# First modulation before the first FFN, the other seven vectors summed during it

## The reference

```python
m_lat = (jax.nn.silu(c) @ w_mod[l] + b_mod[l]).reshape(B, 1, N_MOD, D_MODEL)
m_ctx = (jax.nn.silu(c_ctx) @ w_mod[l] + b_mod[l]).reshape(N_MOD, D_MODEL)
def half_ffn(h, mod, i, g, w_up, w_down):
    shift, scale, gate = mod[..., 3 * i, :], mod[..., 3 * i + 1, :], mod[..., 3 * i + 2, :]
    return h + 0.5 * gate * swiglu(modulate(rms_norm(h, g), shift, scale), w_up, w_down)
h = half_ffn(h, m_lat, 0, g_norm[l, 0], w_ffn_up[l, 0], w_ffn_down[l, 0])
hc = half_ffn(hc, m_ctx, 0, g_norm[l, 0], w_ffn_up[l, 0], w_ffn_down[l, 0])
n_lat = modulate(rms_norm(h, g_norm[l, 1]), m_lat[..., 3, :], m_lat[..., 4, :])
h = h + m_lat[..., 5, :] * merge_branches(...)
h = half_ffn(h, m_lat, 2, g_norm[l, 2], w_ffn_up[l, 1], w_ffn_down[l, 1])
```

## Time and profile before

| | us |
|---|---|
| median of 3 runs | 3064.5 |
| lowest, highest | 3062.27, 3064.74 |
| profiled execution: span from first to last instruction | 3062.6 |
| TensorE busy in it | 2882.0 (94%) |
| DVE busy | 1494.6 (49%) |
| ScalarE busy | 556.8 (18%) |
| GpSimd busy | 69.0 (2%) |
| TensorE's mean granted clock | 0.959 |

### The profile page before, as it was taken

The page is one execution under the profiler, slowest core; times in us unless marked ns, Lnnn a source line. Parts: engine busy times, 40 slices in busy tenths (PEclk is TensorE's granted clock), DMA queues, the critical chain, the costliest instruction groups (busy, mean ns, idle before and its releaser), DMA issues. The chain is left out here.

```text
span 3062.6 us, 35904 instructions
## 1 busy us (share of the span) xinstructions
PE 2882.0 (94%) x14410; PEld 2300.6 (75%) x14410; DVE 1494.6 (49%) x2399; ACT 556.8 (18%) x1039; POOL 69.0 (2%) x104
## 2 busy tenths in 40 slices
PE   8999999999999999999956859998999999999998
PEld 3588888888888787888245637776877888888887
DVE  5544444444444711111696378886745444444444
ACT  3200000000000411111422337774011000000002
POOL 0000000000000000000000001221000000000001
PEclk9999999999999999999875669999999999999999
DMA  8511111111111211233400100001430111111111
GB/s 290 164 35 42 34 41 34 41 34 41 34 41 42 77 43 42 86 97 104 141 1 1 42 0 1 1 1 63 129 119 28 48 48 48 48 48 44 46 55 69
DMA packets 190653, 176.15 MB, mean 58 GB/s; under 512 B 5805, under 2 KB 147290, under 8 KB 190554
## 3 DMA queue, kind: packets, MB, share of 16 engines
q1 hardware_dynamic: 184794, 164.29, 17.3%
q10 hardware_dynamic: 5760, 10.49, 0.9%
HBM read 155.89 MB, written 18.87 MB: 57 GB/s over the span
## 5 line engine op out<-in xcount | busy, mean ns | idle before, releaser
L209 PE MATMUL psum<-nh,wh 128*128 128x512 f32 (+2 forms) x1688 | 613.3, 363 | 1.9 <-DVE wl L186 1.4
L210 PE MATMUL psum<-nl,wh 128*128 128x512 f32 (+2 forms) x1688 | 612.9, 363 | 0.0
L211 PE MATMUL psum<-nh,wl 128*128 128x512 f32 (+2 forms) x1688 | 612.5, 363 | 0.0
L184 DVE CAST wh<-raw 128x1024 fp32r<-128x1024 f32 x175 | 120.2, 687 | 707.8 <-PE psum L211 696.7
L209 PEld LDWEIGHTS psum<-nh,wh 128*128 128x128 f32 (+1 forms) x1688 | 317.1, 188 | 54.2 <-DVE wl L186 1.8
L211 PEld LDWEIGHTS psum<-nh,wl 128*128 128x128 f32 (+1 forms) x1688 | 316.8, 188 | 51.2
L210 PEld LDWEIGHTS psum<-nl,wh 128*128 128x128 f32 (+1 forms) x1688 | 317.1, 188 | 50.6
L717 DVE SCALAR_TENSOR_TENSOR h<-psum,gates,h 128x512 f32<-128x512 f32 (+1 forms) x400 | 271.0, 696 | 143.6 <-PE psum L211 140.5
L209 PE MATMUL psum<-hidh,wh 128*128 128x512 f32 (+1 forms) x880 | 328.2, 373 | 8.0 <-DVE hidl L701 7.6
L685 ACT ACTIVATE silu_a<-psum 128x512 f32<-128x512 f32 (+1 forms) x110 | 61.2, 556 | 1489.9 <-PE psum L211 1489.9
L210 PE MATMUL psum<-hidl,wh 128*128 128x512 f32 (+1 forms) x880 | 324.8, 369 | 0.0
(11 more groups left out here) (241 smaller groups left out, 3399.1 us busy)
## 6 DMA issues: line engine op xcount, KB each, us to landing
raw<-in_w_ffn_up_dram SPq DMA_DIRECT2D x88, 512.0 KB, 3.8
mod_raw<-in_w_mod_dram SPq DMA_DIRECT2D x24, 1024.0 KB, 5.2
raw<-in_w_ffn_down_dram SPq DMA_DIRECT2D x44, 512.0 KB, 3.8
raw<-in_w_in_dram SPq DMA_DIRECT2D x34, 512.0 KB, 3.8
mod_raw_late<-in_w_mod_dram SPq DMA_DIRECT2D x12, 1024.0 KB, 5.2
gates_saved<-staged ACTq DMA_DIRECT2D x40, 256.0 KB, 2.0
merge_gate<-gates_saved SPq DMA_DIRECT2D x8, 1024.0 KB, 5.1
x_rows<-in_x_dram SPq DMA_DIRECT2D x8, 512.0 KB, 7.2
```

The lines of the kernel that those rows point to most:

```text
L184: nc.vector.tensor_copy(wh[:, par, 0:n], raw[:, par, 0:n]).then_inc(panel_split, 1)
L209: pe.matmul(o, hi_w, hi_x, start=first, stop=False)
L210: pe.matmul(o, hi_w, lo_x, start=False, stop=False)
L211: return pe.matmul(o, lo_w, hi_x, start=False, stop=last)
```

## The change

Only the first four blocks (vectors 0 and 1: shift and scale of the first FFN, both samples) are still multiplied by TensorE ahead of the FFN, in eight slots that need no waiting. The norm moves behind them, and the first panels are split before it, so that TensorE's pairs follow the norm block by block. The other seven vectors (e = 0 to 6, numbers 2 to 8) are made by GpSimd in groups 0 to 6 of the first FFN: SP loads 16 parts of 128 x 512 for a vector, GpSimd scales each by silu(c) per partition and adds it up, for vectors e = 0 to 2 also for the context; then TensorE sums the 128 partitions with matmuls against a column of ones, at the head of the group's down panels, and DVE adds the bias (`part_sums`, `part_finish`). Semaphores are shared with later stages, the vector loads move to ScalarE's queue, and the constants of later stages load later. The blocks in the GLA stage are gone. In after's code the L numbers are higher (L184 is L192, L209 is L217, L418 is L502, L428 is L512, L717 is L819).

```diff
--- before.py
+++ after.py
...
-    mod_raw = [at("mod_raw0", 120, [4, 512]), at("mod_raw1", 128, [4, 512]), at("mod_raw2", 164, [4, 512])]
-    mod_raw_late = [at("mod_raw_late0", 140, [4, 512]), at("mod_raw_late1", 172, [4, 512]),
-                    at("mod_raw_late2", 164, [4, 512])]
-    mod_row = at("mod_row", 201, [2, 512])
+    mod_raw = [at(f"mod_raw{n}", kb, [4, 512]) for n, kb in enumerate((120, 128, 164, 80, 88, 96, 104, 112))]
+    mod_row = at("mod_row", 193, [2, 512])
+    acc_lat, acc_ctx = at("acc_lat", 174, [D]), at("acc_ctx", 197, [D])
+    mod_part = [at(f"mod_part{n}", kb, [512]) for n, kb in enumerate((201, 203, 205, 186.5))]
+    part_prod = at("part_prod", 188.5, [512])
...
+    part_loaded, select_loaded = rows_loaded[0:4], rows_loaded[8]
...
+    MOD_FIRST = 4
+    PART_VECS = 7
+    PARTS = 2 * KT
+    def part_both(e):
+        return e < 3
...
-        if p >= 3:
-            sp.wait_ge(mod_product, p - 2)
...
+    def part_load(sp, e, i, begins):
+        k, half = i // 2, i % 2
+        if not (begins and i < 4):
+            sp.wait_ge(lat_added, e * PARTS + i - 3)
+        sp.dma_start(mod_part[i % 4][:, :],
+                     w_mod[0, k * P:(k + 1) * P, bass.ds(e * D + 2 * D + half * 512, 512)])\
+            .then_inc(part_loaded[i % 4], 16)
...
-        sp.dma_start(cst[:, :, :], consts.rearrange("p (n c) -> p n c", c=P)).then_inc(const_loaded, 16)
         for dst, src in vec:
-            sp.dma_start(dst, src).then_inc(vec_loaded, 16)
+            act.dma_start(dst, src).then_inc(vec_loaded, 16)
+    def load_sp(sp):
+        const = consts.rearrange("p (n c) -> p n c", c=P)
+        sp.dma_start(cst[:, 0:K_BLK, :], const[:, 0:K_BLK, :]).then_inc(const_loaded, 16)
         for i in range(TOK // P):
             src = x[0, i * P:(i + 1) * P, :] if i < SEQ // P else ctx_in[0, i * P - SEQ:(i + 1) * P - SEQ, :]
             sp.dma_start(x_rows[:, i, :], src).then_inc(rows_loaded[i], 16)
-        for p in range(MOD_LATE):
+        for p in range(5):
             mod_load(sp, p)
+        for j in range(2):
+            ffn0.load_up(sp, 0, j)
+        for p in range(5, 2 * MOD_FIRST):
+            mod_load(sp, p)
+        sp.wait_ge(FirstNorm.total_done, 3)
+        sp.dma_start(cst[:, K_SEL:N_CONST, :], const[:, K_SEL:N_CONST, :]).then_inc(select_loaded, 16)
...
+    def mod_finish(dve):
+        dve.wait_ge(mod_turned, MOD_FIRST)
+        nc.vector.tensor_tensor(modv[:, 0:16, :], ps[3][:, 0:32].rearrange("p (n s) -> p n s", s=2),
+                                cols_a[:, A_BMOD:A_BMOD + 16].unsqueeze(2).to_broadcast([P, 16, 2]),
+                                ALU.add).then_inc(mod_evac, 1)
+        dve.wait_ge(mod_evac, 1)
+        scale_coef(0, slice(0, 2))
...
+    def parts_pool(pool):
+        pool.wait_ge(silu_c_done, 2)
+        pool.wait_ge(FirstNorm.total_done, 3)
+        lat = ctx = scaled = 0
+        for e in range(PART_VECS):
+            for i in range(PARTS):
+                n, k, cols = e * PARTS + i, i // 2, slice(512 * (i % 2), 512 * (i % 2) + 512)
+                pool.wait_ge(part_loaded[i % 4], 16 * (n // 4 + 2))
+                raw_part = mod_part[i % 4][:, :]
+                if k == 0:
+                    if e >= 1:
+                        pool.wait_ge(sums_done, e)
+                    if part_both(e):
+                        nc.gpsimd.tensor_scalar(acc_ctx[:, cols], raw_part, silu_c[:, k, 1:2], None, ALU.mult)\
+                            .then_inc(ctx_added, 1)
+                        ctx += 1
+                    nc.gpsimd.tensor_scalar(acc_lat[:, cols], raw_part, silu_c[:, k, 0:1], None, ALU.mult)\
+                        .then_inc(lat_added, 1)
+                    lat += 1
+                    continue
+                if part_both(e):
+                    pool.wait_ge(ctx_added, ctx)
+                    nc.gpsimd.tensor_scalar(part_prod[:, :], raw_part, silu_c[:, k, 1:2], None, ALU.mult)\
+                        .then_inc(part_scaled, 1)
+                    scaled += 1
+                nc.gpsimd.tensor_scalar(raw_part, raw_part, silu_c[:, k, 0:1], None, ALU.mult)\
+                    .then_inc(part_scaled, 1)
+                scaled += 1
+                if part_both(e):
+                    pool.wait_ge(part_scaled, scaled - 1)
+                    pool.wait_ge(ctx_added, ctx - 1)
+                    nc.gpsimd.tensor_tensor(acc_ctx[:, cols], acc_ctx[:, cols], part_prod[:, :], ALU.add)\
+                        .then_inc(ctx_added, 1)
+                    ctx += 1
+                pool.wait_ge(part_scaled, scaled)
+                pool.wait_ge(lat_added, lat - 1)
+                nc.gpsimd.tensor_tensor(acc_lat[:, cols], acc_lat[:, cols], raw_part, ALU.add).then_inc(lat_added, 1)
+                lat += 1
+    def part_sums(pe, e, both):
+        pe.wait_ge(lat_added, e * PARTS + PARTS)
+        if both:
+            pe.wait_ge(ctx_added, e * PARTS + PARTS)
+        for s, acc in enumerate((acc_lat, acc_ctx) if both else (acc_lat,)):
+            for q in range(KT):
+                mm = pe.matmul(ps[7][:, KT * s + q:KT * s + q + 1], acc[:, q * P:(q + 1) * P], ones[:, 0:1],
+                               start=True, stop=True)
+        mm.then_inc(sums_done, 1)
+    def part_finish(dve, e, both):
+        n = 2 if both else 1
+        dve.wait_ge(sums_done, e + 1)
+        nc.vector.tensor_tensor(modv[:, bass.ds(e * 8 + 16, 8), 0:n],
+                                ps[7][:, 0:KT * n].rearrange("p (s n) -> p n s", s=n),
+                                cols_a[:, bass.ds(e * 8 + (A_BMOD + 16), 8)].unsqueeze(2).to_broadcast([P, 8, n]),
+                                ALU.add).then_inc(sums_evac, 1)
...
+            loops = [(1, 3, "both"), (3, PART_VECS, "lat"), (PART_VECS, self.GROUPS - 1, None)]
+            for a, b, parts in loops if self.with_parts else [(1, self.GROUPS - 1, None)]:
+                with eng.Fori(a, b) as g:
+                    body(g, False, False, parts)
...
+        PART_LOADS = ((0, 0, 4, 4, 4, 4), (3, 3, 3, 3, 2, 2))
...
+            def body(g, first, last, parts):
+                i = 0
+                for j in range(6):
+                    if j < 4:
+                        if not (first and self.with_parts and j < 2):
+                            self.load_up(sp, g, j)
+                    else:
+                        load_panel(sp, self.panel(g, j), raw[:, self.slot(j), :].rearrange("p (k n) -> p k n", k=2),
+                                   down[:, bass.ds(g * 2, 2), (j - 4) * 512:(j - 3) * 512])
+                    for _ in range(self.PART_LOADS[0 if first else 1][j] if parts else 0):
+                        part_load(sp, g, i, first)
+                        i += 1
...
+                if parts:
+                    part_sums(pe, g, parts == "both")
...
+                            if parts and i == 1:
+                                pe.wait_ge(sums_evac, g + 1)
...
+                if parts:
+                    part_finish(dve, g, parts == "both")
+                    if first:
+                        dve.wait_ge(sums_evac, 1)
+                        gate_coef(0, slice(0, 2))
+                        dve.wait_ge(coef_done, 2)
...
-        dve.wait_ge(coef_done, 4)
+        dve.wait_ge(sums_evac, PART_VECS)
+        scale_coef(1, slice(0, 2))
+        gate_coef(1, slice(0, 1))
+        scale_coef(2, slice(0, 1))
+        gate_coef(2, slice(0, 1))
+        dve.wait_ge(coef_done, 6)
...
-        mod_load(sp, MOD_LATE)
-        mod_load(sp, MOD_LATE + 1)
+        sp.dma_start(cst[:, K_BLK:K_SEL, :], consts.rearrange("p (n c) -> p n c", c=P)[:, K_BLK:K_SEL, :])\
+            .then_inc(mask_loaded, 16)
         sp.wait_ge(dec_zero, 1)
         sp.dma_start(wdec[0:RANK, 0:256], w_decay[0, 0]).then_inc(dec_loaded, 16)
         sp.dma_start(wdec[RANK:2 * RANK, 256:512], w_decay[0, 1]).then_inc(dec_loaded, 16)
-        for n in range(4):
-            sp.wait_ge(saved[n], 16 * 10)
-        for p in range(MOD_LATE + 2, 2 * MOD_BLOCKS):
-            mod_load(sp, p)
...
+            pe.wait_ge(g_kk, 2 * d + 2)
             if s >= 2:
                 pe.wait_ge(g_kcopy, s - 1)
             for t in range(2):
@@ -1109,10 +1218,8 @@
             mm.then_inc(g_kt, 1)
         pe.wait_ge(g_vcopy, N_CHUNKS)
-        mod_pe(pe, range(2 * MOD_GROUP, MOD_BLOCKS), range(2 * MOD_GROUP, MOD_BLOCKS))
-        pe.wait_ge(g_kk, 4)
+        pe.wait_ge(g_min, len(dec_units))
         turn_keys(0)
-        pe.wait_ge(mod_evac, 3)
         for s, (_, ch, _, _) in enumerate(steps):
             if s + 1 < len(steps):
...
-            mod_copy(dve, 2 * MOD_GROUP + j)
...
-        for n in range(2 * MOD_GROUP + 4, MOD_BLOCKS):
-            mod_copy(dve, n)
-        mod_finish(dve, 2)
...
+    def first_mods_pe(pe, c):
+        mod_block(pe, c + 1)
+        if c >= 1:
+            mod_turn(pe, c - 1)
...
-        mod_pe(pe, range(0, 2), ())
-        norm0.pe(pe, lambda c: mod_pe(pe, (c + 2,), (c,)))
```

(32 more changed lines are left out.)

114 lines of the change are left out of this document (49 added, 65 removed).

## The result

The changed kernel takes 3116.5 us (median of 4 runs, 3115.05 to 3118.06), the kernel before 3063.4 beside it: a ratio of 1.0178, interval 1.0165 to 1.0190. It is 53 us slower; the prediction said 3078, 13.5 slower, in a range of 3032 to 3098.

The account below looks back on a forecast made before the run. TensorE, busy 100.00 of 100.00 us in the first FFN, was taken as the bound. Front -17, sums +18.5, clock +5, splits +11, middle -4 gave +13.5 on 3064.5: 3078 us, range 3032 to 3098.

Parts of the forecast that it names:

- front, to the first sums: Start of the first FFN: first sums earlier by 44.7 us without contention, 13 with turns; 17 us gain taken.
- waits at later vectors: First FFN, later groups: GpSimd needs 76 of 83 us per vector, so TensorE never waits; 0 us.
- sums at the full clock: TensorE's added 128-partition sums in the first FFN: 160 records at 0.116, nothing hides them; 18.5 us more.
- clock: Light TensorE work lowers the clock at the three long sums, 1.7 us each; 5 us more.
- splits in the down phase: DVE's panel splits wait for GpSimd and hold up TensorE, 0.9 us, twice in six groups; 11 us more.
- middle: Linear-attention stage without the last six modulation blocks: keys and transposes 6.3 us earlier, partly lost to low clock; gain 4.
- TensorE now follows it unit by unit: First FFN's start: TensorE's paired first panels keep pace with the norm and end at 90.6 instead of 145.3.
- the turns in the norm: GpSimd and DVE alternate on SBUF work in the first norm: 25 us longer, norm end 114.
- the scaling at 0.61: GpSimd's scaling of a 512-column part: 0.61 us taken, between bounds 0.61 and 1.28; vector for both samples 59.4.
- the norm's start: First norm, behind four modulation blocks on TensorE: starts at 55.8 us, not 71.64.
- the addition: GpSimd's addition of a 512-column part: 1.28 us, bounded by rows for 1024 and 256 elements.
- rival B: GpSimd too slow: scaling 1.28, waits of 13 us at vectors 1 and 2, front 11 more, 3115; chance 0.14.

Follow-up runs that it names:

- early_free: Changed kernel with ScalarE's permission for TensorE's first three banks given right behind the norm's three square roots, ahead of its 24 other activations: 3093.7 us, ratio 1.0104.
- tt_scale: Changed kernel with GpSimd's scalings written as a product of two tensors instead of a tensor with a scalar by pointer: 3101.0 us, ratio 1.0125.
- short_parts: Changed kernel with GpSimd's scalings and additions working on 8 of 512 columns, order, waits and loads kept, result not the reference's: 3053.5 us, ratio 0.9968.
- short_parts_early_free: Changed kernel with both GpSimd's parts on 8 of 512 columns and ScalarE's bank permission ahead of the norm's activations: 3035.5 us, ratio 0.9915.
- the experiment: Kernel before without its last six modulation blocks in the linear-attention stage, result not the reference's: 3057.9 us against 3061.9, ratio 0.9988.

## Why the prediction was wrong

Term by term, in the prediction's sum and as the trace has it:

| term | predicted | measured | from |
|---|---|---|---|
| front, to the first sums | -17 | +9.4 | 183.13 - 173.70 |
| waits at later vectors | 0 | +8.9 | 4.47 + 4.46 |
| sums at the full clock | +18.5 | +17.7 | 3 x 3.5 + 4 x 1.8 |
| clock | +5 | +17 | 5.5 + 6.2 + 5.1 behind the start of each long sum |
| splits in the down phase | +11 | +3.6 | the six waits |
| middle | -4 | -5.5 | 59.3 - 53.8 |
| sum | +13.5 | +51 | span: +50.4 |

The clock's 17 us are my estimate: each window's length times one minus its granted clock (183.13 to 196, clock 0.57; 280.76 to 294, 0.53; 378.28 to 392, 0.63). Some 10 of them are in the sums (7.0 instead of 3.5), the rest in the down phases behind. That the sum meets the span so closely is in part luck. Ahead of the middle the terms make 56.6 of the 59.3 us by which TensorE is behind there, so 2.7 have no term; and from the 53.8 at the first state update to the 50.4 at the end another 3.4 come back, in the rest of the GLA and in attention, whose cause stays open.

**The step that failed first:** "TensorE now follows it unit by unit". DVE's grant of the banks had been moved ahead of the norm, and I took that for all of it. TensorE needs two grants; the other is one line on ScalarE, which the diff doesn't touch, behind 24 activations that each wait for the norm. Shown by `early_free`: 23 us less, 3093.7, which lies inside the stated range. With that one line moved the first sums stand at 159.83, so the front's term is -13.9 where the prediction had -17 (GpSimd done at 161). That closeness is luck: the scaling was more than twice as long as taken, and the turns in the norm cost 14.6 instead of 25. Reading the instructions ahead of the releasing one on *every* engine that releases, not only on the engine that the diff edits, would have found it.

**The step that failed by size:** the scaling at 0.61. I had bounds of 0.61 and 1.28 and chose the lower, as the row with one input. The truth, 1.56, is above both. The upper bound was none: it took an instruction with two tensors for the dearest, and the scalar by pointer was dearer. `tt_scale` and `short_parts` show what hangs on it. With 1.56 and 1.26 a vector for both samples is 32 x 1.56 + 28 x 1.26 = 85 us alone, not 59.4, before any turns; the room is 85. So the waits at the second and third sums exist, and the one at the first is 20.81 even with the grant moved (23.65 in the changed kernel), where the prediction had 10 without turns and 17 with them. The Trainium skill (GPSIMD Engine Reference, 3.1) has 769 ns as the best case of a tight loop at 512 elements, and names no instruction for it. Neither form here comes near it, with 1557 by pointer and 1032 with the column as a second tensor, and the trace decides.

**The clock** was the third: priced at 1.7 behind each long sum, on the thought that light work lowers it. For sums without a wait that was right in kind and nearly in size. In six versions 14 long sums were reached without a wait; behind 13 of them the level fell with TensorE busy all the time, and the loss, estimated as above, was 1.7 us in eight and 3.4 in five (`short_parts`: 1.7, 3.4, 1.7; `short_parts_early_free`: 0, 1.7, 1.7). None of the shorter sums, of 16 records, was followed by it. What the prediction had at nothing is the wait: behind the waits of 4.5 us and more the level was low through nearly all of the long sums and until 11 or 12 us behind their start, a loss of 5.1 to 6.2 each. So about 10 of the 17 us hang on the second step and go with the waits; the other 7 are the sums' own (6.8 in `short_parts`), where 5 were forecast.

**Turns were right in kind.** DVE's instructions between SBUF tensors lengthen beside GpSimd, those with a PSUM operand don't. Between 200 and 800 us, the changed kernel and then `short_parts`:

```profile
L819 DVE SCALAR_TENSOR_TENSOR h<-psum,gates,h 128x512 f32<-128x512 f32 x109 | 80.5, 748 | 65.7 <-PE psum L219 65.7
L194 DVE TENSOR_TENSOR wl<-raw,wh 128x1024 fp32r<-128x1024 f32 x41 | 60.8, 1482 | 1.4
L192 DVE CAST wh<-raw 128x1024 fp32r<-128x1024 f32 x41 | 34.4, 840 | 146.0 <-PE psum L219 145.5 <-issue 0.3
...
L798 DVE TENSOR_TENSOR prod<-silu_a,psum 128x512 f32<-128x512 f32 x26 | 17.9, 689 | 85.3 <-PE psum L219 85.3
```

```profile
L823 DVE SCALAR_TENSOR_TENSOR h<-psum,gates,h 128x512 f32<-128x512 f32 x112 | 82.7, 749 | 66.2 <-PE psum L219 66.1
L194 DVE TENSOR_TENSOR wl<-raw,wh 128x1024 fp32r<-128x1024 f32 x42 | 51.5, 1226 | 1.4
L192 DVE CAST wh<-raw 128x1024 fp32r<-128x1024 f32 x42 | 29.0, 689 | 153.8 <-PE psum L219 153.1 <-issue 0.3
...
L802 DVE TENSOR_TENSOR prod<-silu_a,psum 128x512 f32<-128x512 f32 x28 | 19.3, 689 | 100.3 <-PE psum L219 100.3
```

The residual (748 against 749) and the product with PSUM (689, 689) are untouched; the split's subtraction grows from 1226 to 1482 and its cast from 689 to 840. The size in the norm was 14.6 us (46.1 busy in the four groups of the changed kernel, 31.5 in those of `short_parts`), not 25. The two don't strictly take turns: the 28 GpSimd instructions there would take 16 x 1.56 + 12 x 1.26 = 40.1 us alone, so DVE lost some four tenths of that. GpSimd lost time as well, they took 48.0. Still, DVE's 31.5 and GpSimd's 40.1 make 71.6 one behind the other, and both were done within 49 us. Of the splits in the down phase six made TensorE wait, 0.6 each, where I had twelve at 0.9. The Trainium skill (SBUF — State Buffer, Who interferes with whom) has an exclusive lock between the two engines for such forms; the trace agrees on which forms suffer, and shows a smaller price than one whole instruction behind the other would have.

**Right:** the norm's start (55.8 forecast, 55.39), the addition (1.28, 1.26), the sums, the middle (-4 by the experiment), no wait for the vectors for latents. That a time near that of rival B (3115) came out is chance: its path had 13 us of wait at each of two vectors and TensorE following the norm.

## What to carry to other kernels

A consumer's start is the latest of all the grants that it waits for; follow each back on the engine that gives it, also where the diff is silent. An operation that no trace shows, on a slow engine, with slack of a few per cent behind it, should be bounded from above by something that it can't exceed, or the plan should leave it the slack: the version with two groups of time for a vector did not care which form was used. A wait of TensorE can cost more than its length: here sums behind a wait of 4.5 us lost 5 to 6 more by the low clock, and sums without a wait 1.7 or 3.4. And a helper engine that reads SBUF beside DVE's SBUF work can delay the engine that everything waits for; here the first sums came 7.4 us earlier when GpSimd started behind the norm.
